# A hybrid decoder layer on one core: warm-up products dropped, small sample products spread over slots and padded, row scales moved to VectorE

## The reference: what is computed

```python
h = _rmsnorm(x, norm_g)
proj = jnp.einsum('btd,de->bte', h, w_in)
qa, ka, va, ga, xb, gb, qc, kc, vc, gc = jnp.split(proj, SPLIT_IDX, axis=-1)
...
mixed = jnp.concatenate([oa * jax.nn.silu(ga), ob * jax.nn.silu(gb), oc * jax.nn.silu(gc)], axis=-1)
y = x + jnp.einsum('bte,ed->btd', mixed, w_out)
```

## Time and profile before

| | us |
|---|---|
| median of three runs | 734.37 |
| lowest, highest | 730.46, 735.66 |
| the profiled execution | 740.12 |
| its span, first to last instruction | 738.3 |
| TensorE busy | 720.0 (98%) |
| VectorE, ScalarE, GpSimd busy | 325.9, 273.5, 137.8 |
| mean granted TensorE clock | 0.974 |

### The profile page before, as it was taken

How to read it: one execution, slowest core, us unless ns; L and a number is a source line. 1 busy time by engine, 2 the same in 40 slices (tenths; PEclk the granted TensorE clock), 3 DMA queues, 4 the chain that set the end, 5 groups by cost and what they waited for, 6 DMA issues and landing times. The chain is left out here.

```text
span 738.3 us, 11451 instructions
## 1 busy us (share of the span) xinstructions
PE 720.0 (98%) x4460; PEld 662.5 (90%) x4460; DVE 325.9 (44%) x720; ACT 273.5 (37%) x691; POOL 137.8 (19%) x237
## 2 busy tenths in 40 slices
PE   7999999999999989899999998999999999999998
PEld 7999999989998979799999998999899988888884
DVE  5362452423333165787752385318723573111102
ACT  6552332322222135556626455325453351000000
POOL 0001170615353152213122221112100000000000
PEclk8999999989998999999999999999999999999999
DMA  8402104112120310101131011031011451122101
GB/s 307 151 1 87 58 2 184 46 62 58 42 78 6 113 57 1 58 1 58 58 108 46 28 59 29 4 105 59 1 30 58 157 186 57 72 81 76 58 36 36
DMA packets 24081, 50.04 MB, mean 68 GB/s; under 512 B 1752, under 2 KB 16088, under 8 KB 21820
## 3 DMA queue, kind: packets, MB, share of 16 engines
q1 hardware_dynamic: 24028, 49.31, 19.5%
HBM read 42.22 MB, written 9.12 MB: 70 GB/s over the span
## 5 line engine op out<-in xcount | busy, mean ns | idle before, releaser
L401 PE MATMUL proj<-big 128*128 128x352 f32 (+1 forms) x952 | 309.4, 325 | 8.9 <-DVE big L1167 5.9
L402 PE MATMUL proj<-big 128*128 128x352 f32 (+1 forms) x952 | 296.6, 312 | 0.0
L403 PE MATMUL proj<-big 128*128 128x352 f32 (+1 forms) x952 | 296.2, 311 | 0.0
L401 PEld LDWEIGHTS proj<-big 128*128 128x128 f32 x952 | 184.4, 194 | 19.3 <-issue 7.1
L402 PEld LDWEIGHTS proj<-big 128*128 128x128 f32 x952 | 184.8, 194 | 0.6
L403 PEld LDWEIGHTS proj<-big 128*128 128x128 f32 x952 | 184.3, 194 | 0.0
L1167 DVE TENSOR_TENSOR big<-raw,big 128x512 fp32r<-128x512 f32 (+2 forms) x72 | 49.8, 704 | 54.2 <-ACT big L804 54.0
L401 PE MATMUL branch<-big,m_parts 128*128 128x512 f32 x144 | 56.8, 395 | 0.0
L402 PE MATMUL branch<-big,m_parts 128*128 128x512 f32 x144 | 56.8, 394 | 0.0
L403 PE MATMUL branch<-big,m_parts 128*128 128x512 f32 x144 | 56.8, 394 | 0.0
L1412 DVE TENSOR_TENSOR m_parts<-mixed,m_parts 128x1024 fp32r<-128x1024 f32 (+3 forms) x18 | 15.3, 888 | 82.5 <-ACT m_parts L1096 82.5
(11 more groups left out here) (237 smaller groups left out, 1019.9 us busy)
## 6 DMA issues: line engine op xcount, KB each, us to landing
raw<-w_units SPq DMA_DIRECT2D x17, 1024.0 KB, 4.8
x_res<-x_prompt SPq DMA_DIRECT2D x8, 512.0 KB, 4.1
out_y_prompt<-y_out SPq DMA_DIRECT2D x8, 512.0 KB, 2.9
raw<-w_out SPq DMA_DIRECT2D x6, 512.0 KB, 4.1
y_out<-w_out SPq DMA_DIRECT2D x6, 512.0 KB, 4.1
mixed<-x_T SPq DMA_DIRECT2D x8, 352.0 KB, 8.9
s<-state_ret SPq DMA_DIRECT2D x4, 512.0 KB, 3.9
out_s_ret<-s SPq DMA_DIRECT2D x4, 512.0 KB, 3.2
```

What stands on the lines that cost most here:

```text
L401: pe.matmul(out, a_lo, b_hi, start=first, stop=False)
L402: pe.matmul(out, a_hi, b_lo, start=False, stop=False)
L403: return pe.matmul(out, a_hi, b_hi, start=False, stop=last)
```

## The change

The nine constant products at the beginning are gone, and the first unit's pieces hold two blocks k each. A retention head's sample work at slot 9 is split: the 32-row product and four of the eight state products stay there, four and the product with v_sel go to slot 10 (`ret_two_more`). v_sel and k_dec get 128 rows, the rows from 32 up being zero, so that the products with v_sel have 128 rows. `samp_scores` is split over slots 21 and 22, `samp_values` over 30, 31 and 32, and `samp_pturn` moves from slot 29 to 28. GpSimd's row scales are gone: VectorE multiplies xb by rb as it takes it from the bank (`xb_row`), in place of ScalarE's copy, and scales the gate rows (`gate_row`, at ROW_AT). ScalarE squares aa, which VectorE did. The tables for conv, gates, silu and weight splitting have new numbers: in units 7 to 11 the pieces of the next unit's weights are split at slots 2 to 5 or 0 to 3.

```diff
-FIRST_PIECES = ((0, 1), (1, 2), (2, 5), (5, 8))
+FIRST_PIECES = ((0, 2), (2, 4), (4, 6), (6, 8))
...
-            v_sel = sb("v_sel", [NS, DB, DH], scope=r)
+            v_sel = sb("v_sel", [P, DB, DH], scope=r)
...
-        LRU_AT = {name: {(7 + (7 + first + 11 * f) // 12, (7 + first + 11 * f) % 12): f for f in range(H)}
-                  for name, first in (("conv", 0), ("gates", 5), ("m2", 9), ("sqrt", 10), ("scan", 11))}
+        LRU_AT = {name: {divmod(slot, 12): f for f, slot in enumerate(slots)} for name, slots in (
+            ("conv", (90, 98, 108, 119)), ("gates", (95, 106, 117, 128)), ("m2", (100, 111, 122, 133)),
+            ("sqrt", (101, 112, 123, 134)), ("scan", (102, 113, 124, 135)))}
...
-        SILU_AT = {(7, 4): 0, (7, 5): 1, (9, 4): 2, (10, 0): 3, (12, 1): 4, (12, 2): 5, (12, 3): 6, (12, 4): 7}
-        W_AT = (3, 5, 7, 9)
+        ROW_AT = {(6, 9): 0, (7, 1): 1, (9, 9): 2, (10, 1): 3, (11, 9): 4, (11, 10): 5, (12, 2): 6, (12, 4): 7}
+        SILU_AT = {(7, 3): 0, (7, 4): 1, (10, 4): 2, (10, 5): 3, (12, 4): 4, (12, 5): 5, (12, 6): 6, (12, 7): 7}
+
+        def w_at(u):
+            return (2, 3, 4, 5) if u == 7 else (0, 1, 2, 3) if 8 <= u <= 11 else (3, 5, 7, 9)
...
-                pe.wait_ge(S_["ones_set"], 1)
-                for _ in range(WARM):
-                    pe.matmul(bb[1][:, 0:P], ones[:], ones[:], start=True, stop=True)
...
+            def ret_two_more(m):
+
+                hd = m // 9
+                samp_out(m, range(DB // 2, DB)).then_inc(S_["o_done"], 1)
+                pe.wait_ge(S_["kdec_set"], m + 1)
+                pe.wait_ge(S_["s_set"], m)
+                pe.wait_ge(S_["vsel_set"], DB * (hd + 1))
+                pe.matmul(bb[3][:, :], k_dec[:, m % 2, :], v_sel[:, 0:4, :].rearrange("p b d -> p (b d)"),
+                          start=True, stop=True).then_inc(S_["kv_done"], 1)
...
-                if s == 29:
+                if s == 28:
                     samp_pturn(half)
-                if s == 31:
-                    samp_values(half)
+                if s in (30, 31, 32):
+                    samp_values(half, s - 30)
...
+                act.wait_ge(S_["exp_set"], 2 * f + 2)
+                act.activation(rg, aa[:], ACT.Square).then_inc(S_["a2_set"], 1)
...
+            def gate_row(r):
+                u = UNITS.index(("gB" if r < 4 else "gC", r % 4 // 2))
+                dve.wait_ge(S_["act_freed"], freed(u, 3 * (r % 2) + 2)[1])
+                dve.tensor_tensor(mixed[:, 4 + r, :], mixed[:, 4 + r, :], rb[:], ALU.mult).then_inc(S_["row_set"], 1)
+
+            def xb_row(u, j):
...
+                dve.wait_ge(S_["proj_done"], g + 1)
+                if c == 2:
+                    dve.tensor_tensor(xb[:, i, 3 + SEQ:].rearrange("p (b i) -> p b i", b=DB)[:, :, 3:7],
+                                      bank[:, n:CH].rearrange("p (b i) -> p b i", b=DB),
+                                      rb[:, SEQ:TOK].rearrange("p (b i) -> p b i", b=DB), ALU.mult)
+                dve.tensor_tensor(xb[:, i, 3 + c * CH:3 + c * CH + n], bank[:, 0:n], rb[:, c * CH:c * CH + n],
+                                  ALU.mult).then_inc(S_["xb_set"], 1)
...
-            xb_scale(0)
-            gate_row(6, 0)
-            gate_row(6, 1)
-            for f in range(1, H):
-                xb_scale(f)
-            for u in (9, 10, 11):
-                for mt in range(2):
-                    gate_row(u, mt)
```

More of the change, by code:

```diff
@@ L75, in freed @@
         return "mix_g", 6 * i + j + 1
-    return "act_freed", sum(UNITS[v][0] not in ("kvC", "qC", "gA") for v, _ in GROUPS[:FIRST_GROUP[u] + j + 1])
+    if kind == "xb":
+        return "xb_set", 6 * i + j + 1
+    return "act_freed", sum(UNITS[v][0] not in ("kvC", "qC", "gA", "xb") for v, _ in GROUPS[:FIRST_GROUP[u] + j + 1])
 K_ORDER = [*range(H, KM), *range(H)]
@@ L94 @@
 N_CR = 1316
+M_PAD = 168
 C_BIASS, C_BIAS = 0, 2 * AKEYS
@@ L520, in ret_two @@
                     pe.wait_ge(S_["s0_in"], 16 * (hd + 1))
-                    mm = pe.matmul(o[:, 0:NS], v, sT[0:n, m % 2, 0:n], start=True, stop=False,
-                                   skip_group_check=True)
-                    for b in range(DB):
-                        cols = slice(b * DS, (b + 1) * DS)
-                        mm = pe.matmul(o[:, cols], s0[:, b, :], q_dec[:, m % 2, cols], start=False,
-                                       stop=(b == DB - 1), skip_group_check=True)
+                    pe.matmul(o[:, 0:NS], v, sT[0:n, m % 2, 0:n], start=True, stop=False, skip_group_check=True)
+                    samp_out(m, range(0, DB // 2))
+                    return
                 mm.then_inc(S_["o_done"], 1)
@@ L657, in sample_q, with samp_scores @@
                 return qT[:, (9 * half + NT) % 2, 0:2 * NS].rearrange("p (g b i) -> p b g i", g=2, b=DB)
-            def samp_scores(half):
-                pe.wait_ge(S_["qT_set"], 9 * half + 9)
-                pe.wait_ge(S_["kc_copied"], 2 * half + 2)
+            def samp_scores(half, part):
+                if part == 0:
+                    pe.wait_ge(S_["qT_set"], 9 * half + 9)
+                    pe.wait_ge(S_["kc_copied"], 2 * half + 2)
                 q = sample_q(half)
-                for b in range(DB):
+                for b in range(4 * part, 4 * part + 4):
                     pe.matmul(bb[4][:, 8 * b:8 * b + 8], kcT[:, b, :], q[:, b], start=(b == 0), stop=True,
                               skip_group_check=True)
+                if part == 0:
+                    return
                 mm = pe.matmul(bb[4][0:NS, 2 * NS:4 * NS], kT[:, half, SEQ:TOK], q, start=False, stop=True,
@@ L682, in samp_pturn, with samp_values @@
                 pe.transpose(bb[4][0:NS, 64:128], pn, ident[0:64, 0:64]).then_inc(S_["spT_done"], 1)
-            def samp_values(half):
-                pe.wait_ge(S_["spT_set"], half + 1)
-                pe.wait_ge(S_["vcache_in"], 16 * (half + 1))
-                pe.matmul(bb[4][:, 0:64], v_c[0:NS, half, NT, :], kcT[0:NS, 4, 64:128], start=True, stop=False,
-                          skip_group_check=True)
-                for b in range(DB):
+            def samp_values(half, part):
+                if part == 0:
+                    pe.wait_ge(S_["spT_set"], half + 1)
+                    pe.wait_ge(S_["vcache_in"], 16 * (half + 1))
+                    pe.matmul(bb[4][:, 0:64], v_c[0:NS, half, NT, :], kcT[0:NS, 4, 64:128], start=True, stop=False,
+                              skip_group_check=True)
+                for b in ((0, 1), (2, 3, 4), (5, 6, 7))[part]:
                     mm = pe.matmul(bb[4][:, 8 * b:8 * b + 8], cache[:, b, :], kcT[:, 4, 8 * b:8 * b + 8],
                                    start=False, stop=(b == DB - 1), skip_group_check=True)
-                mm.then_inc(S_["sav_done"], 1)
+                if part == 2:
+                    mm.then_inc(S_["sav_done"], 1)
             def att_side(half, s):
@@ L720, in side @@
                         ret_two(base + s - 1)
+                    if s == 10:
+                        ret_two_more(base + NT)
                     if s < 9:
@@ L1213, in sample_eps @@
                 link(dve.tensor_scalar(erow[:], erow[:], EPS, None, ALU.mult))
+            def gate_row(r):
[3 more added lines that the diff above has]
+            def xb_row(u, j):
+                g, f, c = FIRST_GROUP[u] + j, 2 * UNITS[u][1] + j // 3, j % 3
+                i, n = f % 2, min(CH, SEQ - c * CH)
+                bank = proj_bank(g)
+                if f == 0 and c == 0:
+                    dve.wait_ge(S_["mix_a"], 36)
+                    dve.wait_ge(S_["stored_ret"], 32 * H)
+                if f < 2 and c == 0:
+                    dve.memset(xb[:, i, 0:3], 0.0)
+                dve.wait_ge(S_["proj_done"], g + 1)
[5 more added lines that the diff above has]
+                                  ALU.mult).then_inc(S_["xb_set"], 1)
             def ga_row(u, j):
```

110 lines of the change are left out of this document (44 added, 66 removed).

## The result

The changed kernel takes 711.06 us, the median of four runs (710.43 to 711.55); the kernel before, on the same chip, 733.24 us (730.46 to 735.66). The ratio is 0.970, interval 0.966 to 0.974: 3.0% faster.

A forecast was written before the change was run, and what follows sets the result against it. TensorE bounds the kernel, busy 720.0 of 738.3 us, with its clock and waits to be read. Sum from the profiled execution: 740.1 - 14.3 - 5.9 + 0.6 + 1.0 - 0.9 - 2.2 = 718.4 us, range 713 to 726.

The forecast's parts named there:

- padding costs nothing: Retention heads' v_sel products: padding to 128 rows costs nothing on TensorE, 0.90 us for 512 columns against 1.89 with 32 rows.
- Clock: Heads, `samp_values` and two waits: all seven stretches at 0.50 go, 14.3 us gained (8.0, 3.2, 3.2); bounds 0 and 14.3.
- Waits for weights: Start of units 8 and 9: both TensorE waits for the weights' low part go, 5.9 us gained; bounds 0 and 5.9.
- New wait for a bank: Units 7 and 8, VectorE now empties the banks: TensorE waits 0.6 us behind the scan; ends 0 and 5.7.
- Turn of the probabilities: Attention, `samp_pturn` one slot earlier: TensorE waits 1.0 us for the sample probabilities; bounds 0 and 1.4.
- Unit 12: TensorE's wait for a key's turn, behind ScalarE's table load and silu, goes: 0.9 us gained (0 to 0.9).
- The start: First block: first product at 7.3, done at 17.5 us, gain 2.2; bounds a gain of 4.8, a loss of 1.8.
- the whole first block would be at 1.2 GHz: Start, without warm-up: first block done at 21.5 us; as a rival 4 us more, 722.4 us, chance 0.05.
- the small products are not what lowers the clock: Heads and `samp_values`: spreading does nothing, other gains stay; 729.5 us, within 1% of the median; chance 0.07.
- Some falls stay: Heads and `samp_values`: a spread batch can still tip the clock, half of 11.2 us stays; +5.6, 724 us; chance 0.15.
- VectorE's queue holds the banks: Recurrence: slow `conv` or scan, or late ScalarE; wait 3 to 5.7 us, one clock fall; about 724 us; chance 0.10.
- slower: Heads and `samp_values`: spreading lengthens the thin stretch, clock falls, 44 us more; 762 us, slower by 3.8%; chance 0.02.

The follow-up runs named there:

- a_pad8: The changed kernel with the 8 unused columns of before ahead of m_parts, not 168: 713.91 us, ratio 0.969.
- a_together: The changed kernel with the sample products in one batch again (slots 9, 22 and 31), still padded to 128 rows: 718.42 us, ratio 0.977.
- a_32rows: The changed kernel, sample products still spread, but the two products with v_sel use 32 rows again: 713.39 us, ratio 0.970.
- b_w_at: The kernel before with only the changed kernel's slots for the weight pieces in units 7 to 11; GpSimd still scales: 732.68 us, ratio 0.996.
- a_w3579: The changed kernel with the next unit's weight pieces at slots 3, 5, 7 and 9 in every unit, as before: 712.68 us, ratio 0.968.
- a_pturn29: The changed kernel with the turn of the sample probabilities at slot 29 again, not 28: 709.82 us, ratio 0.964.
- a_pieces: The changed kernel with the first unit's pieces of 1, 1, 3 and 3 blocks again, without constant products: 711.80 us, ratio 0.966.
- b_pad168: The kernel before with 168 unused columns ahead of m_parts and not 8: 733.75 us against 735.31 before, ratio 0.998.

## Why the prediction was wrong

The main mechanisms, the clock and the waits for weights, were right in kind. The time fell out of the range because one edit, the place of m_parts, was not in the sum (3.25 us), and because three terms were too small: the heads ("padding costs nothing"), units 7 to 10 with a wait that did not come, and the attention. With the old place of m_parts the changed kernel takes 713.91 us (a_pad8), which is just inside the range. By the steps of the prediction:

1. *Clock.* Right. No stretch of 0.50 behind a head, `samp_values` or a wait; a_together brings three back at 1.6 us each. The three heads gave 9.8 us, not 8.0. That the padding "costs nothing on TensorE" was wrong on the other side: a_32rows has the full clock too and takes 110.7 us for units 4 to 6, which is 7.8 below the kernel before, near the 8.0 of the term; the other 2.0 are the padding. I had costed the padded product and never the seam between 32 and 128 rows that goes away. In unit 3 the padding only takes back what the spread 32-row products cost (39.56 before, 40.05 with 32 rows, 39.48 after). The falls behind `samp_values` came out at their size in unit 17 (1.58); in unit 14 the 1.2 us are the fall, less the new wait, plus a wait of 0.45 for pT that no step had. Unit 16 lost one too; a_together has both again, so they went with the spreading of `samp_scores`.
2. *Waits for weights.* The size was right, 5.9 us and no wait left; the cause only in part. The table alone moves the wait (b_w_at), and with the old table there is one of 1.4 us at another unit (a_w3579).
3. *New wait for a bank.* It did not come, and this is where I chose wrongly between bounds of 0 and 5.7. I took the scan's chain at 7.1 us from the trace before. VectorE's order of time in the changed kernel answers to L1361 to L1370 there:

```profile
278.18 1.26 DVE L1389 TENSOR_TENSOR cv<-cv,rg 128x1056 f32<-128x1056 f32 x1
279.47 0.17 DVE L1390 TENSOR_TENSOR ig<-aa,st_T 128x8 f32<-128x8 f32 x1
...
280.02 2.36 DVE L1393 TENSOR_TENSOR_SCAN tt<-aa,cv 128x1056 f32<-128x1056 f32 x1
282.41 0.17 DVE L1394 COPY tails<-tt 128x8 f32<-128x8 f32 x1
282.56 1.25 DVE L1398 TENSOR_TENSOR mixed<-mixed,tt 128x1056 f32<-128x1056 f32 x1
```

   It takes 5.7 us. The first large operation and the scan have their old length (1.26, 2.36), the small ones do not. In the kernel before, while GpSimd ran its row scales (the rows of POOL), the same ones were as below; the last row is the same operation one round later, with GpSimd idle:

```profile
297.97 2.12 POOL L1652 TENSOR_TENSOR xb<-xb,rb 128x352 f32<-128x352 f32 x2 [6.55 <-ACT xb L882]
...
298.68 0.66 DVE L1362 TENSOR_TENSOR ig<-aa,st_T 128x8 f32<-128x8 f32 x1
299.38 0.74 DVE L1363 TENSOR_TENSOR cv<-cv,ig 128x8 f32<-128x8 f32 x1
...
300.48 2.71 POOL L1652 TENSOR_TENSOR xb<-xb,rb 128x320 f32<-128x320 f32 x1 [0.39 <-ACT xb L882]
...
302.68 0.54 DVE L1366 COPY tails<-tt 128x8 f32<-128x8 f32 x1
...
326.56 0.17 DVE L1362 TENSOR_TENSOR ig<-aa,st_T 128x8 f32<-128x8 f32 x1
```

   That last row means that the trace before held the answer. In the other three of its four rounds the small operations take 0.17 us each, and in two of them the chain from L1361 to the end of L1370 takes 5.6 us with GpSimd idle throughout; I had read the one round that ran beside GpSimd's row scales.

   The row behind the scan was done at 284.2 and its bank wanted at 286.2, a margin of 2 us where my times had TensorE 0.4 us short (taken as 0.6). The scan's chain makes 1.4 of that difference. I had written that GpSimd "has nothing to do here now", used it to set the slow price of `conv` aside, and did not apply it to the scan. The remaining 0.6 us of these units (0.4 of it in unit 10) I did not test.
4. *Turn of the probabilities.* Right: a wait of 0.9 for 1.0, worth 0.97 (a_pturn29).
5. *Unit 12.* Gone, 0.63 for 0.9.
6. *The start.* As forecast in this pair of profiles: first product 7.52 us for 7.3, fast from 12.6 for 12.9, first block done at 17.6 for 17.5, unit 1 earlier by 2.2. That it fits to 0.1 is luck: in the nine profiles with this start the pace rose 2.9 to 5.1 us behind the first product, where I had 5.6, and with the old start unit 1 began at 35.10, 31.98 and 33.96 us in three profiles, with the new one at 31.4 to 32.9 in nine, 32.1 in the mean, which makes the gain 1.6. The pieces alone are worth 0 to 0.8 (a_pieces), the constant products nothing that shows over several executions. The Trainium skill ("TensorE: Matmul & The Clock Gate", "Why this matters for your kernels") advises to warm up before a matmul is measured, since one measures the low clock otherwise. Two profiles with constant products agree in that the first product of data was fast (7.13 and 7.12, the second of them not for long), two do not (fast from 10.4 and from 13.0), and the medians, 710.33 and 710.38, show no gain. That the whole first block would be at 1.2 GHz without a warm-up was my reading of that advice and goes further than it; 17 of the block's 48 products were slow.
7. *What no step had:* the place of m_parts, 3.25 us. It is the largest single miss, and only a complete reading of the diff would have raised the question; I saw nothing in the trace before that pointed to it, since all 576 products were slow alike.

The gap between sum and span adds up: 3.25 from m_parts, 1.8 at the heads, 1.2 in units 7 to 10 and 0.7 in the attention make 7.0, of 28.8 - 21.7 = 7.1.

Of the rivals, "the small products are not what lowers the clock" is refuted by a_together: three falls with TensorE busy throughout, by nothing but their place in the order. In the same table of the Trainium skill's page ("TensorE: Matmul & The Clock Gate", "Why this matters for your kernels"), long idle gaps between bursts are what throws the clock back. The fall behind the wait of 3.0 us in b_w_at agrees; those in a_together show that it also falls without one. "Some falls stay", "VectorE's queue holds the banks" and "slower" did not happen in any profile of the changed kernel.

## What to carry to other kernels

Go through every line of a diff, also where a size of an unused tile changes, and give each a price or a bound; where a tile moves, let the bounds hold a small change of pace for all that reads it. When a change takes an engine out of a stretch, take the durations of its neighbours from a stretch in which that engine was idle; the trace before may well hold one, as here. And what a start-up trick yields must be read from several executions: four profiles with the same constant products put the start of unit 1 anywhere from 30.5 to 33.5 us.

## What the runs showed of the hardware that I had not expected

- The pace of 512-column products depends on where the stationary operand lies in the partition: 0.227 or 0.232 us apart, 3.25 us over 576 products, with the clock at 1.00 in both cases. Four places were tried (pads of 8, 40, 72 and 168 columns: slow, fast, slow, fast).
- A product with 32 rows between products with 128 rows costs about 0.27 us more than one padded to 128, although the profile gives both the same length (1.12 and 1.10 us for the pair).
- Operations of VectorE (8 columns) that take 0.17 us with GpSimd idle took 0.54 to 0.74 while GpSimd worked on whole rows. Large ones are not spared: in these rows it was the one that started later, on either engine, that got longer. The scan started 0.2 us ahead of a row of GpSimd and kept its 2.36 us; that row took 2.71, against 2.12 for the two ahead of it together. And in the last round of the kernel before, L1370 started just behind a gate row of GpSimd and took 3.51 us for its 1.25:

```profile
373.06 2.47 POOL L1644 TENSOR_TENSOR mixed<-mixed,rb 128x1056 f32<-128x1056 f32 x1 [8.01 <-ACT mixed L869]
...
373.13 3.51 DVE L1370 TENSOR_TENSOR mixed<-mixed,tt 128x1056 f32<-128x1056 f32 x1
```

- The clock falls behind a dense run of small products without any idle time, and in one kernel behind some of the batches and not behind others: a_together lost it at three of six, and b_pad168 lost it in unit 3, where the kernel before with the same products did not.
- The column of the granted clock can read 1.00 while products come at the pace of 0.50, as in the first 5 us of data: the trace has no record of the clock yet (the first is at 12.63 us in the changed kernel).
